# Two blocks of a transformer in one kernel: where ScalarE's squares stand, second weight chunks split by halves, and a place of their own for the experts' closing down rows

## The reference

```python
def swiglu(x, wg, wu, wd):
    return (jax.nn.silu(x @ wg) * (x @ wu)) @ wd          # widths 1024 -> 2816 -> 1024

for i in range(2):                                         # first block
    x = layer_norm(ALPHA * x + hybrid_mixer(x, ...), ln1_g[i], ln1_b[i])
    f = swiglu(x, ...) if i == 0 else moe_swiglu(x, ...)   # dense, then 8 experts, top 2
    x = layer_norm(ALPHA * x + f, ln2_g[i], ln2_b[i])
for l in range(2):                                         # second block
    h = h + 0.5 * rmsnorm(swiglu_2(rmsnorm(h, ffn1_pre_g[l]), ...), ffn1_post_g[l])
    h = h + rmsnorm(mixer(rmsnorm(h, mix_pre_g[l])) @ w_out[l], mix_post_g[l])
    h = h + 0.5 * rmsnorm(swiglu_2(rmsnorm(h, ffn2_pre_g[l]), ...), ffn2_post_g[l])

def rmsnorm(x, g):
    return x * rsqrt(mean(x * x, axis=-1) + EPS) * g
```

## Time and profile before

| what | value |
|---|---|
| median of 3 runs | 2621.59 us (2620.32 to 2627.24) |
| the profiled execution | 2625.35 us, its span 2623.5 us |
| TensorE | busy 2531.9 us, 97% of the span |
| VectorE | busy 1789.2 us, 68% |
| ScalarE | busy 1399.2 us, 53% |
| GpSimd | busy 199.4 us, 8% |
| loads | 592.14 MB, mean 226 GB/s |
| the chain that ended last | TensorE 68%, VectorE 8%, ScalarE 4%, issue 2%, DMA 1% |

### The profile page before, as it was taken

The page is one execution under the profiler, slowest core; times in us unless marked ns, Lnnn a source line. Parts: engine busy times, 40 slices in busy tenths (PEclk is TensorE's granted clock), DMA queues, the critical chain, the costliest instruction groups (busy, mean ns, idle before and its releaser), DMA issues.

```text
span 2623.5 us, 32752 instructions
## 1 busy us (share of the span) xinstructions
PE 2531.9 (97%) x12074; PEld 2082.1 (79%) x12074; DVE 1789.2 (68%) x1742; ACT 1399.2 (53%) x1517; POOL 199.4 (8%) x271
## 2 busy tenths in 40 slices
PE   7899998999999999999899999999999999999999
PEld 5778876788888888888788887777888888777787
DVE  4564465788888889889755557785555565778644
ACT  4544445567766766767644454544444345454543
POOL 3000020100000000000033010000004201000000
PEclk9899999999999999999999999999999999999999
DMA  8255552489989989989776353345538644335551
GB/s 266 80 201 192 191 164 81 182 352 357 354 341 352 352 342 358 355 341 360 287 224 235 145 184 129 138 179 216 183 138 277 224 149 177 135 132 190 211 192 64
DMA packets 88136, 592.14 MB, mean 226 GB/s; under 512 B 11304, under 2 KB 11488, under 8 KB 20320
## 3 DMA queue, kind: packets, MB, share of 16 engines
q1 hardware_dynamic: 77472, 558.99, 56.3%
q0 software_dynamic: 10560, 31.74, 4.6%
HBM read 585.36 MB, written 5.32 MB: 225 GB/s over the span
## 4 chain that ended last, share of the span: by engine, by line
PE 68%; DVE 8%; ACT 4%; issue 2%; DMA 1%; POOL 1%; SPq 0%; DVEq 0%; ACTq 0%; POOLq 0%
PE pp L608 14%; PE pp L610 14%; PE pp L609 14%; PE acc L610 6%; PE acc L608 6%; PE acc L609 6%; DVE lo_a L2563 3%; PE tp L813 1%; DMA raw_a<-in_moe_gu 1%; PE acc L758 1%; ACT hi_a L1421 1%; PE acc L948 1%; PE tp L620 1%; PE tp L981 1%; PE acc L969 1%
## 5 line engine op out<-in xcount | busy, mean ns | idle before, releaser
L608 PE MATMUL pp<-hi_a,uT_hi 128*128 128x512 f32 (+1 forms) x2152 | 862.3, 401 | 15.2 <-DVE lo_a L2563 5.8
L610 PE MATMUL pp<-hi_a,uT_lo 128*128 128x512 f32 (+1 forms) x2152 | 841.6, 391 | 0.0
L609 PE MATMUL pp<-lo_a,uT_hi 128*128 128x512 f32 (+1 forms) x2152 | 840.4, 391 | 0.0
L2070 DVE TENSOR_TENSOR lo_a<-raw_a,hi_a 128x2048 fp32r<-128x2048 f32 x282 | 648.8, 2301 | 125.6 <-ACT hi_a L1480 125.1
L1480 ACT ACTIVATE hi_a<-raw_a 128x2048 fp32r<-128x2048 f32 x282 | 537.8, 1909 | 9.6 <-DMA raw_a<-in_moe_gu 9.0
L608 PEld LDWEIGHTS pp<-hi_a,uT_hi 128*128 128x128 f32 x2152 | 407.7, 189 | 98.4 <-issue 11.0
L610 PEld LDWEIGHTS pp<-hi_a,uT_lo 128*128 128x128 f32 x2152 | 407.2, 189 | 87.1
L609 PEld LDWEIGHTS pp<-lo_a,uT_hi 128*128 128x128 f32 x2152 | 408.2, 190 | 78.0
L609 PE MATMUL acc<-lo_b,hT_hi 128*128 128x512 f32 x792 | 308.6, 390 | 0.0
L2103 DVE TENSOR_TENSOR lo_b<-raw_b,hi_b 128x2048 fp32r<-128x2048 f32 x115 | 265.5, 2308 | 47.5 <-ACT hi_b L1500 46.4
L608 PE MATMUL acc<-hi_b,hT_hi 128*128 128x512 f32 x572 | 223.4, 391 | 1.4 <-DVE lo_b L2103 1.4
(11 more groups left out here) (284 smaller groups left out, 2827.0 us busy)
## 6 DMA issues: line engine op xcount, KB each, us to landing
raw_a<-in_moe_gu SPq DMA_DIRECT2D x176, 1024.0 KB, 6.5
raw_b<-in_moe_wd SPq DMA_DIRECT2D x88, 1024.0 KB, 8.4
raw_a<-in_ffn_w_gu SPq DMA_DIRECT2D x88, 1024.0 KB, 6.7
raw_a<-in_w_in SPq DMA_DIRECT2D x72, 1024.0 KB, 6.9
raw_b<-in_ffn_w_down SPq DMA_DIRECT2D x44, 1024.0 KB, 5.0
raw_a<-in_ffn_gu SPq DMA_DIRECT2D x22, 1024.0 KB, 6.4
raw_a<-in_w_out SPq DMA_DIRECT2D x16, 1024.0 KB, 6.4
raw_a<-in_w_branch SPq DMA_DIRECT2D x12, 1024.0 KB, 6.3
```

Of the source, the lines that this page charges most:

```text
L608: nc.tensor.matmul(out_ap, l_hi, r_hi, start=start, stop=False, skip_group_check=True)
L609: nc.tensor.matmul(out_ap, l_hi, r_lo, start=False, stop=False, skip_group_check=True)
L610: return nc.tensor.matmul(out_ap, l_lo, r_hi, start=False, stop=stop, skip_group_check=True)
L2070: ins = nc.vector.tensor_tensor(lo_a[:, slot, cs], raw_a[:, slot, cs], hi_a[:, slot, cs].bitcast(F32), ALU.subtract)
```

## The change

1. The last expert's closing down rows get a place of their own, raw_c (128 x 2048), which lies over sc and pT, with a semaphore s_blast. SyncE issues their load right behind the last but one down rows, with no wait in front, and ahead(1) right after. ScalarE and VectorE read raw_c in place of raw_b's slot; VectorE now waits for s_bused itself before it writes lo_b's slot.
2. ScalarE's halves move: the second half of the dense stage's chunk 0 comes at the end of the last but one body, the first half of its chunk 1 into the last body, followed by a Square of one element; only the second half of chunk 1 stays behind y_hi.
3. After the experts, row_squares for both tiles comes in front of hi_tile(1).
4. Second chunks by halves: out_chunk(True) (in both layers of the first block) and across(1.0, True) use hi_halves, VectorE lo_halves. In across the first half comes before row_squares(1) and hi_tile(1), the second half behind them.
5. In the stick-breaking heads branch(0, 0, 256) of head 1 moves from item(1, 0) to item(1, 1), which is behind pair().

```diff
+        with nc.sbuf_tensor("raw_c", [P, 2048], F32) as raw_c:
+            pass
         sc = sb("sc", [P, 2, TT, S])
         pT = sb("pT", [P, 2, TT, S])
...
+                def last_rows():
+                    sp.dma_start(raw_c[:, :], weights[1][bass.ds((experts - 1) * P, P), bass.ds((N_FCH - 1) * 2048, 2048)]) \
+                      .then_inc(s_blast, 16)
...
                     if last and experts > 1:
                         ahead(0)
-                        for r in range(2):
-                            side_b(Chunk(half + 4, odd + 1 + r), e, N_FCH - 2 + r)
+                        side_b(Chunk(half + 4, odd + 1), e, N_FCH - 2)
+                        last_rows()
                         ahead(1)
                         return
...
-            def hi_halves(size=4096):
+            def hi_halves(size=4096, parts=(0, 1)):
                 slot = n["a"] % 2
-                landed[slot] += 32
-                act.wait_ge(s_al[slot], landed[slot])
-                for part in range(2):
+                if 0 in parts:
+                    landed[slot] += 32
+                    act.wait_ge(s_al[slot], landed[slot])
+                for part in parts:
...
                 if last:
-                    hi_chunk_a((s_acc[1], n["acc"] + 1))
+                    act.wait_ge(s_acc[1], n["acc"] + 1)
+                    hi_halves()
...
-                def hi_rows(c, dst):
+                def hi_rows(c, dst, src=None):
                     slot = (b0 - 1 + c.rest) % 2
-                    act.wait_ge(s_bl[slot], c.turns(0) * 16 + (base_b[slot] + 16))
-                    nc.scalar.activation(dst[:, :], raw_b[:, slot, :], ACT.Copy).then_inc(s_bhi, 1)
+                    if src is None:
+                        act.wait_ge(s_bl[slot], c.turns(0) * 16 + (base_b[slot] + 16))
+                    else:
+                        act.wait_ge(s_blast, 16)
+                    nc.scalar.activation(dst[:, :], raw_b[:, slot, :] if src is None else src, ACT.Copy) \
+                      .then_inc(s_bhi, 1)
...
                     if sparse and is_last_rows(e, j):
                         silu(c)
                         hi_hidden(c)
-                        hi_next(Chunk(c.half, c.rest - 1), 1)
+                        hi_next(c, 0)
+                        nc.scalar.activation(stat[:, 146:147], zcol, ACT.Square)
                         return
                     if sparse and is_last(e) and isinstance(j, int) and j == N_FCH - 2:
                         silu(c)
                         hi_next(c, 0)
                         down_side(c)
-                        hi_rows(c.next(), hi_c)
+                        hi_rows(c.next(), hi_c, raw_c[:, :])
+                        hi_next(c, 1)
                         return
...
                             split_y_half(e.odd, h)
-                        for part in range(2):
-                            hi_next(c, part)
+                        hi_next(c, 1)
...
-                    if it == 1 and part == 0:
+                    if it == 1 and part == 1:
                         act.wait_ge(s_plo, i + 1)
                         branch(0, 0, 256)
...
                 n["acc"] += 1
+                n["x"] = 0
                 for tt in range(TT):
                     norm_squares(tt)
+                    if i + 1 == N_LAYERS and tt == 1:
+                        for other in range(TT):
+                            row_squares(other)
                     hi_tile(tt, i + 1 == N_LAYERS)
-            n["x"] = 0
-            for tt in range(TT):
-                row_squares(tt)
...
                     row_squares(0)
                     if chunk:
-                        hi_chunk_a()
+                        hi_halves(parts=(0,))
+                        row_squares(1)
                     hi_tile(1, True)
-                    row_squares(1)
+                    if chunk:
+                        hi_halves(parts=(1,))
+                    else:
+                        row_squares(1)
...
-                def lo_b_rows(c, spare=False):
+                def lo_b_rows(c, spare=False, own=False):
                     dve.wait_ge(s_bhi, c.at(b0 + 1))
                     slot = (b0 + c.rest) % 2
                     hb = hi_c if slot and not sparse or spare else hi_b
-                    nc.vector.tensor_tensor(lo_b[:, slot, :], raw_b[:, slot, :], hb[:, :].bitcast(F32),
+                    src = raw_b[:, slot, :]
+                    if own:
+                        dve.wait_ge(s_bused, c.at(bu0 - 1))
+                        src = raw_c[:, :]
+                    nc.vector.tensor_tensor(lo_b[:, slot, :], src, hb[:, :].bitcast(F32),
                                             ALU.subtract).then_inc(s_blo, 1)
...
                 if i == 0:
-                    lo_chunk_a()
+                    lo_halves()
...
                     signal(s_ppv)
-                    lo_chunk_a()
+                    lo_halves()
                     gathered_opening()
...
                 across(3 * l + 2)
-                lo_chunk_a()
+                lo_halves()
                 rest = ffn(1, l + 1 == N_LAYERS, scaled=True)
```

More of the change, by code:

```diff
@@ L294, in program @@
         s_accfront = [sem("s_accfront0"), sem("s_accfront1")]
+        s_blast = sem("s_blast")
         s_bhi = sem("s_bhi")
@@ L1422, in hi_halves @@
                       .then_inc((s_ahalf, s_ahi)[part], 1)
-                n["a"] += 1
+                if 1 in parts:
+                    n["a"] += 1
             def front_chunk():
@@ L1510, in down_side @@
                     act.wait_ge(s_bused, c.at(bu0 if sparse else bu0 - 1))
-                    hi_rows(c, hi_c if slot and not sparse else hi_b)
+                    hi_rows(c, hi_c if slot and not sparse else hi_b, src)
                 def head():
@@ L1541, in body @@
                         hi_next(c, 0)
-                        down_side(c)
+                        down_side(c, raw_c[:, :] if is_last_rows(e, j) else None)
                     hi_next(c, 1)
@@ L1561, in ffn @@
                     landed[(a1 + c) % 2] += 32
-                    landed_b[(b0 - 1 + c) % 2] += 16
+                    if experts == 1 or c + 1 < k:
+                        landed_b[(b0 - 1 + c) % 2] += 16
                 n["bu"] += k - 1
@@ L2054, in ffn @@
                 a1, b0, g0, hi0, ppa0, half0 = n["a"], n["b"], n["g"], n["thi"], n["ppa"], n["half"]
+                bu0 = n["bu"] + 2
                 tiles = 1 if sparse else TT
@@ L2134, in body @@
                         turned(c)
-                        lo_b_rows(c)
+                        lo_b_rows(c, own=is_last_rows(e, j))
                     if sparse and isinstance(j, int) and j in (2, 3) and not is_first(e):
@@ L2164, in ffn @@
                 n["b"] += k
+                n["bu"] += k - 1
                 n["g"] += k
```

4 lines of the change are left out of this document (2 added, 2 removed).

## The result

The changed kernel takes 2602.47 us, the median of three runs (2602.46 to 2605.99), against 2621.59: the ratio is 0.9929, with a 95% interval of 0.9915 to 0.9943. That is 19.1 us less; the forecast was 15.5 us less, 2606.1, with a range of 2600 to 2616. The profiled execution took 2602.47 us (span 2600.7) at a mean granted clock of 0.990; the one of before took 2625.35 at 0.986, so the two traces lie 22.9 us apart.

The account below looks back on a forecast made before the run. TensorE, busy 97%, was the bound, so gains come from its idle gaps and half clock: 7.1 + 1.6 + 3.4 + 1.9 + 1.6 - 0.1 = 15.5 us, from 2621.59 to 2606.1, range 2600 to 2616.

Parts of the forecast that it names:

- Closing rows: Experts' end: raw_c's load lands at 1283.4, TensorE turns at 1288.3, its wait falls from 2.92 to 0.4; 2.5 us gained.
- Rival (a): Experts' end: closing rows share full DMA engines, ScalarE stays late; seam 3.4 instead of 7.1, total 2609.8; chance 0.14.
- The table load ahead of y_hi: Last expert: 1.28 us Square table load precedes y_hi, which starts at 1292.6, 3.7 earlier; norm's Square then gains 2.3.
- Rival (b): Before y_hi: the switch to Square's table holds ScalarE longer than its row; gain 14.1, 2607.5; chance 0.12.
- Norm, root and second chunk: Behind the experts: gained rows start at 1303.6, 5.8 us earlier; second chunk 1.3 earlier; whole seam 7.1, bounds 3.4 and 7.8.
- Dense stages: Second chunks by halves: 1.6 us gained in the first block, 1.7 in each of the second block's two layers.
- Heads: Stick-breaking heads: turned pair's copy starts 0.94 us earlier in each of two layers; 1.9 gained, bounds 0 and 1.9.
- The clock: Two half-clock stretches behind second chunks: both may go (3.4) or others come (-1.6); 1.6 us taken.
- more than 18, when both stretches go: Whole kernel: case of a gain above 18 us, with both half-clock stretches gone; chance 0.03.
- the one with 0.56: Whole kernel: the forecast case itself, a gain of 13 to 18 us; chance 0.56.
- (c): Seams: gains are given back to later waits or half-clock stretches; gain 5.4, 2616.2, within 0.3%; chance 0.12.
- (d): Last expert: half copy ahead of y_hi waits for its weights; slower, 2630 if it waited 24 us; chance 0.03 with its like.

Follow-up runs that it names:

- the experiment with parts 1 and 2 alone: Kernel before with only raw_c for the closing down rows, ScalarE's halves reordered and the one-element Square; 2616.52 us, ratio 0.9979.
- the held load: Changed kernel, but SyncE waits for the old s_bused value before raw_c's load; 2606.14 us, ratio 0.995 of before.
- part 3 alone: Kernel before with only both tiles' row_squares put ahead of hi_tile(1) after the experts; 2619.38 us, ratio 0.9997.
- The two last experiments: Kernel before with dense-stage squares and hi_tile(1) ahead of whole copies, 2625.03 us; kernel before with second chunks by halves, squares still last, 2615.99 us.
- the repeated comparison: The unaltered changed kernel timed again against the kernel before; 2603.94 us, ratio 0.9937.

## Why the prediction was right, and where its steps were off

**Closing rows, right.** They were to land at 1283.4 in the old time, bounded by 1283.0. The load landed 10.5 us after its issue (forecast 10.4), and the copy starts at 1273.17, which is 1283.34; in the experiment with parts 1 and 2 alone it waits 0.50 for the load. The turn was to be at 1288.3 and was at 1288.2, with 0.31 of wait against 0.4. Rival (a), that the load would come no earlier because the queue is full, is refuted by the same rows, though the full queue took most of the lead (8.0 us at the issue, 2.4 at the landing), and the held load brings back 2.49 us of wait on ScalarE and 2.51 before the turn.

**The table load ahead of y_hi, wrong.** I had put the load of 1.28 us on ScalarE's path by means of the one-element Square, so that ScalarE was free only at 1292.6. There is no load ahead of that Square. ScalarE stands ready 1.16 us early, TensorE is the bound, and y_hi comes 3.90 us behind the turn and not 4.3: at 1292.1 in the old time, a gain of 4.25 where 3.7 was forecast. The same step then credited the norm's Square with having its table already. It hasn't: the load stands behind the branch with the Square and without it. The Square begins at 1297.3 in the old time instead of 1303.23: 5.9 earlier, of which 4.25 comes from y_hi; 1.7 is left where the forecast had 2.3. Rival (b), a drain besides the load, lost its object. The Trainium skill (ScalarE: Activation LUTs, What ACT_TABLE_LOAD costs) has 1283 ns for the load, and the rows of 1.28 agree; of its drain, the row at 1285.85, 0.14 us behind the copy's end with Square starting at the load's end, shows nothing.

**Norm, root and second chunk, right by a different sum.** The gained rows were to start at 1303.6 and start at 1303.5. TensorE's transposes ended about when forecast (first turn of x at 1302.7, forecast 1303.0), but what the rows wait for is VectorE, whose own work ends just ahead of them. The second chunk's wait went to 0.44 (forecast 0.4), bound by VectorE's halves as said. The seam gave 8.1 us, forecast 7.1, range 3.4 to 7.8. It is above the range by 0.3, and the excess of 1.0 is a sum of errors that partly cancel: 0.55 more up to y_hi, 0.4 less from there to the dense stage's first product (1.7 against 2.1), and 0.94 within the first chunk that the forecast had at nothing. In before the clock is 0.54 over 1313 to 1316 us, behind a gap of 2.06 in front of the first chunk; after, that gap is 0.38 and the clock full. The gap doesn't decide it: with part 3 alone it is 2.06 too and the clock stays full. That the idle transposes begin "a fixed 2.2 us" behind the last product is not quite so either: the gap is 2.19 to 2.74 in the twelve traces.

**Dense stages, right.** First block: wait 0.61, forecast 0.65; 1.65 us gained, forecast 1.6. Second block: waits 0.50 and 0.48, 1.71 gained in each layer, forecast 1.7. The add takes 0.22 us instead of 4.09. The side remark that a root which comes too late "gets in between the two halves" was wrong: it gets half in. The two last experiments show that the halves alone leave 1.75 of 2.01 and that the squares first, with whole copies behind the rows, make it 3.32; early squares with the copy at its old place are untested. The Trainium skill (SBUF — State Buffer, SBUF: two separate sides) says that a VectorE instruction with two SBUF inputs keeps GpSimd off the shared port pair for its whole length; the trace agrees, one instruction at a time (4.09 beside 4.42, 1.95 and 2.61 beside the two halves of 4.48 together).

**Heads, right.** 0.94 and 0.94, forecast 1.9 for both, though the plain medians can't show it (at equal clock 1.7, plus or minus 1.1).

**The clock, too small.** I took 1.6 us, where I had written that both stretches may go, 3.4. Both went, and more with them. The waits alone give 12.2 us in the trace, forecast 12.7 (13.9 less the 1.2 that I took for a faster way from the turn to y_hi); the fit over all runs gives 13.6 at equal clock, plus or minus 1.5. So the shortfall of the forecast is here: about 3.9 us in repeated runs, and some 10 between the two profiled executions, of which the one of before was a low-clock one (0.986 against a mean of 0.9875). The gain of 19.1 us thus fell in my case "more than 18, when both stretches go", to which I gave 0.03, and not in the one with 0.56; the repeated comparison, 16.1, lies in that one.

In this pair four places next to an edit can be named where before ran at half clock and after didn't: 1.6 us behind the turn, 1.2 in the first chunk behind the experts, and 1.6 at each of the two stretches that I had in view. They make 6.0 us, 2.3 of the 4 thousandths by which the two executions differ. The twelve traces hold 48 waits before a second chunk. In the 10 us behind each, the clock is 1.00 in all 33 cases with 1.75 us of wait or less. Of the 15 with 2.00 to 3.32 us it is 0.83 or 0.84 in ten and 1.00 in five. So closing such a wait took away what half clock tends to follow, but the wait doesn't decide it: the four waits of 2.00 in the second block's second layer all keep 1.00. This is the window 1785 to 1795 in before and with the squares first, and the same stage with the halves and squares last (second chunk at 1789.17, 1786.38 and 1779.29):

```profile
1785.00:1795.00 10.00, 7.99 (x29) 6.13 (x28) 5.21 (x4) 2.64 (x3) 2.85 (x2) 0.83 0.68 265
```

```profile
1785.00:1795.00 10.00, 8.62 (x33) 7.08 (x34) 4.09 (x5) 1.27 (x3) 0.00 (x0) 0.83 0.80 313
```

```profile
1779.00:1790.00 11.00, 10.71 (x49) 8.90 (x50) 5.62 (x5) 6.25 (x5) 0.00 (x0) 1.00 0.67 278
```

Away from the edits (120 to 150 and 440 to 460 us) such stretches come and go between executions: a stretch of 30 us in the heads, from 5 us behind the first score products of the earlier trace rows on, has 0.83 in before and 0.94 in the changed kernel, but 0.94 also in four experiments without part 5 and 0.89 in one with it. Why a stretch comes in one execution and not in another stays open.

**Rivals (c) and (d).** Nothing that the times can show was given back: the parts add, within 2.8 us. The half copy ahead of y_hi starts at 1278.79 with no wait for its weights, so (d) is nowhere in the trace.

## What to carry to other kernels

When a chain of several engines ends a wait, undo the links together: earlier squares with whole copies behind them made this one longer, halves alone shortened it little, and both took three quarters of it away. A place of its own lets a load go out early, but price it by its landing: 8.0 us earlier at the issue were 2.4 at the landing. Before you charge an engine for a table load, find in the trace which functions follow each other without one, and where a load and an idle gap stand whatever the order of the work. And where the forecast holds a sum of waits, ask of each wait whether a half-clock stretch follows it in the trace, and give that a term with bounds of its own.

## What the runs showed of the hardware that I had not expected

- A Square of one element right behind silu and copies took 0.19 us and no table load, yet a load stands ahead of the same function behind the branch.
- Where the experts' branch ends ScalarE and TensorE each lose some 2 us for which the profile shows no wait: 1.94 us on ScalarE when it has nothing else to do, 2.19 to 2.74 on TensorE in the twelve traces.
- A GpSimd instruction of 128 x 2 elements is held by a running VectorE subtraction until that ends, and the next one by the next: 1.95 and 2.61 us instead of 0.22 and 0.72.
- The 24 idle transposes behind TensorE's gap ran 4.32 us in one trace, 2.84 in another and 5.38 in a third, with gaps of 2.46, 2.42 and 2.59 us ahead: nearly the same idle time may or may not be followed by half clock. At 5.38 they held the norm's rows up by 1.43 us.
- A load of 1.05 MB took 10.5 us from issue to landing when issued 8.0 us earlier and 4.9 when issued late.
- 0.001 of mean clock goes with 1.77 us here (plus or minus 0.19). If TensorE alone set the time it would be 2.6 us (2620 x 0.001), so, as an estimate, about a third of the lost speed costs nothing. The clock is known to three decimals only, which makes the fitted slope somewhat small.
